# One weight item of each mixture loaded as one wide transfer and several eight-partition transfers

## The reference

```python
for e in range(N_EXPERTS):
    h = jax.nn.silu(t @ w_gate[e]) * (t @ w_up[e])
    y = y + combine[:, e:e + 1] * (h @ w_down[e]).astype(jnp.float32)
...
a = jax.nn.silu(jnp.einsum('becd,edf->becf', xs, w_gate)) * jnp.einsum('becd,edf->becf', xs, w_up)
y = jnp.einsum('becf,efd->becd', a, w_down) * g[..., None].astype(h.dtype)
```

## Time and profile before

| | us |
|---|---|
| median of 3 runs | 1846.8 (1843.21 to 1848.1) |
| the profiled execution, span from the first to the last instruction | 1843.4 |
| TensorE busy in it | 1431.2 |

### The profile page before, as it was taken

The page is one execution under the profiler, slowest core; times in us unless marked ns, Lnnn a source line. Parts: engine busy times, 40 slices in busy tenths (PEclk is TensorE's granted clock), DMA queues, the critical chain, the costliest instruction groups (busy, mean ns, idle before and its releaser), DMA issues.

```text
span 1843.4 us, 30528 instructions
## 1 busy us (share of the span) xinstructions
PE 1431.2 (78%) x13618; PEld 824.4 (45%) x13618; DVE 489.0 (27%) x999; ACT 245.8 (13%) x561; POOL 84.3 (5%) x92
## 2 busy tenths in 40 slices
PE   9999887776587999999666656678999756656666
PEld 5456442333243364666334334336867423434333
DVE  5864321111121169942000000004643100000000
ACT  3233210111211122411000000001001000000000
POOL 4100000000000042100000000000000000000000
PEclk9999998888899999999778778789999977887888
DMA  9665999999999996788999999999997999999997
GB/s 366 239 240 233 395 418 427 427 426 426 425 422 422 405 348 243 289 354 369 431 431 429 429 430 431 429 427 391 391 393 317 431 430 430 429 430 431 431 423 330
DMA packets 78031, 717.69 MB, mean 389 GB/s; under 512 B 5064, under 2 KB 9928, under 8 KB 48584
## 3 DMA queue, kind: packets, MB, share of 16 engines
q1 hardware_dynamic: 76336, 712.85, 93.0%
q10 hardware_dynamic: 1560, 2.82, 0.4%
HBM read 714.60 MB, written 1.05 MB: 388 GB/s over the span
## 4 chain that ended last, share of the span: by engine, by line
DMA 50%; PE 39%; DVE 5%; issue 2%; POOL 2%; ACT 1%; SPq 0%; ACTq 0%; DVEq 0%
DMA ring<-in_moe_w_down 33%; PE bank L1787 9%; DMA ring<-in_w_down 8%; PE bank L2680 5%; PE bank L535 4%; DMA ring<-in_attn_w_in 3%; PE bank L1729 3%; DMA ring<-in_moe_w_gate 2%; PE bank L1738 2%; PE bank L1047 2%; PE bank L1016 2%; PE bank L679 2%; DMA room<-in_rows 1%; PE bank L2440 1%; PE bank L1641 1%
## 5 line engine op out<-in xcount | busy, mean ns | idle before, releaser
L1738 PE MATMUL bank<-ring,arena 128*32 128x256 f32 x3840 | 288.2, 465 | 161.4 <-DMA ring<-in_moe_w_up 118.6
L1787 PE MATMUL bank<-ring,arena 128*32 128x256 f32 x2944 | 238.6, 486 | 138.8 <-DMA ring<-in_moe_w_down 113.1
L1738 PEld LDWEIGHTS bank<-ring,arena 128*32 128x32 f32 x3840 | 160.2, 132 | 285.2 <-issue 220.2
L1787 PEld LDWEIGHTS bank<-ring,arena 128*32 128x32 f32 x2944 | 123.7, 137 | 242.1 <-issue 193.1
L1729 PE MATMUL bank<-ring,arena 128*32 128x512 f32 x976 | 131.6, 661 | 64.6 <-ACT arena L1829 32.5
L1860 DVE TENSOR_TENSOR arena<-arena,bank 128x128 f32<-128x128 f32 (+1 forms) x64 | 22.7, 355 | 503.3 <-PE bank L1738 496.3
L535 PE MATMUL bank<-ring,low 128*128 128x512 f32 (+1 forms) x352 | 152.7, 581 | 0.1
L1815 PE MATMUL bank<-arena 32*128 32x256 f32 x1024 | 91.8, 428 | 15.0 <-PE bank L1815 10.6
L1871 ACT ACTIVATE arena<-bank 128x256 f32<-128x256 f32 x64 | 24.6, 385 | 556.6 <-PE bank L1801 554.3
L535 PEld LDWEIGHTS bank<-ring,low 128*128 128x128 f32 x352 | 64.9, 192 | 65.9 <-issue 65.0
L1729 PEld LDWEIGHTS bank<-ring,arena 128*32 128x32 f32 x976 | 27.5, 115 | 144.6 <-issue 63.9
(11 more groups left out here) (324 smaller groups left out, 1343.0 us busy)
## 6 DMA issues: line engine op xcount, KB each, us to landing
ring<-in_moe_w_gate SPq DMA_DIRECT2D x20, 4096.0 KB, 23.7
ring<-in_moe_w_up SPq DMA_DIRECT2D x20, 4096.0 KB, 23.7
ring<-in_moe_w_down SPq DMA_DIRECT2D x20, 4096.0 KB, 23.6
ring<-in_w_gate SPq DMA_DIRECT2D x31, 2048.0 KB, 22.6
ring<-in_w_up SPq DMA_DIRECT2D x30, 2048.0 KB, 23.8
ring<-in_w_down SPq DMA_DIRECT2D x30, 2048.0 KB, 24.5
ring<-in_ada_w SPq DMA_DIRECT2D x24, 2048.0 KB, 13.5
ring<-in_moe_w_up SPq DMA_DIRECT2D x22, 2048.0 KB, 20.8
```

The source lines that it names most:

```text
L1738: last = nc.tensor.matmul(GU[up][32 * j:32 * j + 32, 0:QW], xgT[:, x + kk, a:a + C], w[:, kq, j * QW:(j + 1) * QW], start=(kk == 0), stop= ...
L1787: last = nc.tensor.matmul(z_bank(M)[32 * j:32 * j + 32, 0:QW], act_s[:, kk, :], w[:, kq, j * QW:(j + 1) * QW], start=(kk == 0), stop=(kk = ...
```

## The change

In each mixture one gate item (expert 28 in stage 1, 8 in stage 2, 10 in stage 3) is no longer loaded by one transfer of 128 partitions. Partitions 0 to 79 (stage 1) or 0 to 95 (stages 2 and 3) go by one transfer, which counts up the slot's semaphore, and the rest by six or four transfers of eight partitions each, which count up `low_loaded`. This is the semaphore `half_loaded` under a second name, so the count that the last item waits for is raised. TensorE waits for both semaphores before the item's matmuls. The bytes moved are the same.

```diff
+LOW8 = {1: (28, 6), 2: (8, 4), 3: (10, 4)}
...
+        self.low_expert, self.low_parts = LOW8.get(stage, (None, 0))
...
+        low_loaded = half_loaded
+        low_at = [16 + 16 * sum(LOW8[n][1] for n in range(1, stage + 1)) for stage in range(4)]
+
+        def in_two(M, i):
+            return M.stage and i == place_up(M, M.low_expert, 0, 0)
+
+        def load_in_two(M, dst, src, landed):
+
+            at = P - 8 * M.low_parts
+            nc.sync.dma_start(dst[0:at], src[0:at]).then_inc(landed, 16)
+            for p in range(at, P, 8):
+                nc.sync.dma_start(dst[p:p + 8], src[p:p + 8]).then_inc(low_loaded, 16)
+
         def wait_moe_item(pe, M, i, r, k):
+            if in_two(M, i):
+                pe.wait_ge(low_loaded, low_at[M.stage])
...
-                    pe.wait_ge(half_loaded, 32)
+                    pe.wait_ge(half_loaded, low_at[3] + 16)
...
-                nc.sync.dma_start(ring[slot][:, :, :].rearrange("p a b -> p (a b)").rearrange("p (k n) -> p k n", n=rows_.shape[2]),
-                                  rows_).then_inc(M.arrived[slot], 16)
+                dst = ring[slot][:, :, :].rearrange("p a b -> p (a b)").rearrange("p (k n) -> p k n", n=rows_.shape[2])
+                if in_two(M, i):
+                    load_in_two(M, dst, rows_, M.arrived[slot])
+                    return
+                nc.sync.dma_start(dst, rows_).then_inc(M.arrived[slot], 16)
...
-                nc.sync.dma_start(slots.rearrange("p (k n) -> p k n", n=rows_.shape[2]), rows_).then_inc(arrived[at % SLOTS], 16)
+                dst = slots.rearrange("p (k n) -> p k n", n=rows_.shape[2])
+                if in_two(M, i):
+                    load_in_two(M, dst, rows_, arrived[at % SLOTS])
+                    return
+                nc.sync.dma_start(dst, rows_).then_inc(arrived[at % SLOTS], 16)
```

## The result

The kernel after takes 1911.3 us (median of 4 runs, 1908.4 to 1914.4) against 1846.1 us (median of 4 runs of the kernel before; three of them stood ahead of the prediction, with 1846.8), a ratio of 1.0353 with a 95% interval of 1.0339 to 1.0366. The prediction was 1840.1 us in a range of 1836.5 to 1850. Both the sign and the range are wrong. The profiled execution has a span of 1911.6 us, 68.2 longer than before.

A forecast was written before the change was run, and what follows sets the result against it. Each mixture was taken to last as long as its weights stream, ending with the more loaded DMA engines. 1.83 + 2.44 + 2.44 = 6.7 us off, costs 0.0, gave a 1836.7 us span and 1840.1 us median, range 1836.5 to 1850.

The forecast's parts named there:

- Engines and packets: Pair items in the mixtures: one 32 KB row is one packet, so an eight-row transfer occupies at most eight engines.
- The shift: Changed items: rows moved between engine halves at 26.9 or 25.6 GB/s per engine shift each engine by 1.83 or 2.44 us.
- The terms of 1.83, 2.44 and 2.44 us off: Ends of first, second and third mixture: each comes earlier by its shift, 6.7 us off together.
- The waits that were to end near 642.9 and 1256.7: TensorE's waits at the ends of the first two mixtures, before at 644.72 and 1260.96, would end earlier.
- Which half: Changed items: small transfers fall on the less loaded eight engines, taken by judgment; the other half would end 2.44 us later.
- rival A: Small transfers fall on engines that also fetch instructions; mixtures end 1.83, 2.44, 2.44 us later, 1853.5 us; chance 0.12.
- the light half: Eight of sixteen DMA engines, without instruction fetches, end the third mixture at about 1828.1, a gap of 5.3 us.
- The costs taken as nothing: Fourteen more SyncE issues, TensorE's second wait and added completion packets: -0.1 to +0.5 us in all, taken as 0.0.
- What follows the mixtures: Stretches behind the mixtures and the end after 1835.02 keep their length and only move with the mixtures' ends.
- Cover: DMA queue in the mixtures: 14 us of work stand ahead of an item, against a lead of 5.3 us.
- C: Small transfers are serialized: fourteen at some 2 us each add 28 us, 1875 us; chance 0.02.
- What would show it: Signs in the profile after: earlier wait ends and no half-share tail if right; other tails or share gaps if wrong.

The follow-up runs named there:

- patterns: Separate kernel without compute, loading weights in one row pattern after another, each alone and waited for: eight neighbouring rows 20.9 us, all 128 rows 41.3 us.
- step4_high: Against the changed kernel: small transfers into rows 96 to 127 take every fourth partition, four in every mixture; 1891.8 us, ratio 1.0253 to the kernel before.
- columns_pair: Against the kernel before: changed items cut by columns into two 128-partition transfers, three quarters and one quarter of each row; 1844.7 us, ratio 1.0003.
- stream_pieces: Separate kernel without compute, streaming a divided item among whole 128-row items: 68.0 us with the change's division, 41.2 us with four whole items.

## Why the prediction was wrong

**Engines and packets.** That an eight-row transfer is eight packets on at most eight engines was right. Completion packets are the short ones on the page: 5176 after, 5064 before, 112 more for fourteen more transfers, eight each.

**The shift, the step that failed.** "One engine moves 430 / 16 = 26.9 GB/s when all are busy and 205 / 8 = 25.6 in the tail ... so the shift is 1.83 us and 2.44 us for each engine." Both rates were read in transfers of 128 partitions and used for transfers of 8, 80 and 96. Nothing in the trace of before showed a large transfer of another shape in this queue, and the value should have had a bound from below as the issue cost had. Measured for the same bytes, in the stream: 21.9 us for the four small transfers, in place of 4.9 us of eight engines' time, and 14.6 us for rows 0 to 95, in place of 7.3. The terms of 1.83, 2.44 and 2.44 us off came out as 18.0 (with the stretch behind the first mixture), 21.5 and 27.0 us on. The waits that were to end near 642.9 and 1256.7 ended at 659.7 and 1300.5.

Behind the wrong rate stands a wrong picture. I treated the item as bytes that any engine can take from any other. By the map that `patterns` found, each group of rows has one way with one engine's rate, and a whole item already puts an equal load on every way. Rows given to other engines still go through the same ways, where the engines now meet. So moving rows makes no way's load lighter: it is eight rows for each whole item, whoever carries them. That is a conclusion from the map, not a run of its own; nor did a run try whether another engine could fill a way while the way's own engine fetches instructions. For the wide part, more than half of the price in `step4_high`, the picture is not complete: that it runs at half the rate is measured, why is open.

**Which half.** The whole forecast hung on it, by my words, and so did rival A with 0.12. No run settles which engines fetch instructions, since a shift of 2.4 us never showed under costs of 4 to 27. Whether the light half was the right guess stays open.

**The costs taken as nothing** were right: four issues 1.36 us, hidden behind queued work; the second wait, one more transfer and its completions 0 us (`columns_pair`). The completions of all fourteen were not tried by themselves. What follows the mixtures kept its length less well than I had it: the stretch behind the first grew by 3.0 us in 192, that behind the second by 1.6 in 136, and the last 8.4 us did not change.

**Cover.** "14 us of work stand ahead of it" held for gaps of 5 us. It does not cover an item that needs 27 us more of the queue itself: TensorE waited 22.76 us.

**The rivals.** C, at 0.02, had the right sign and place and a price of 28 us where 66.5 came in the three stage costs. Its mechanism, serialized fixed costs, is refuted by `columns_pair` and by step 4, which changed the price of the third mixture at the same number of transfers (27.0 to 18.1). I dismissed it since "the mixtures stream one item after another at 430 GB/s"; they do so with whole items only. The Trainium skill's rule cited there (DMA: Bandwidth & Descriptors, section "Rules for kernel authors": use one 128-partition transfer rather than two to disjoint halves, which serialize) was good advice here, and the trace agrees: in `patterns` each half took 43.6 us by itself, the two issued together 84.2, all 128 rows in one transfer 41.3. I had taken from it only a fixed cost for each transfer and left out that each half by itself runs at half the rate.

**What would show it.** "Gaps of 1 to 2 us in the share at the changed items (C)" would have missed it: the share had no gap. The rate beside the share shows it.

## What to carry to other kernels

A rate belongs to the shape of the transfer it was read in. Before a stream of 128-partition transfers is cut by partitions, price the new shape by itself: here a 96-row part of an item took 1.5 times as long as the whole item, and eight neighbouring rows moved 50 GB/s, the rate of two engines; a cut along the columns cost nothing. And read the GB/s line together with the DMA share: 0.85 at 125 GB/s was a queue full of slow transfers, which the share alone does not tell from a good stream.

## What the runs showed of the hardware

- Eight rows of 128 KB: 20.9 us as neighbours, 12.7 with step 2, 7.6 with step 4, 12.6 with step 16; the order in on-chip memory counts, not that in the source (20.6 and 7.4 with the two exchanged).
- Rows of 128 KB by number: 32 spread rows 12.5 us, 32 neighbours 22.5 and 22.7, 64 rows 43.6, 128 rows 41.3, all by the load of the busiest way. More than that load explains: 48 rows (80 to 127) and 80 rows (0 to 79) 52.4 each, 96 rows 63.1 (0 to 95) and 62.7 (32 to 127), 112 rows 65.4. Engines that meet one after the other on several ways might do that; it was not tried by itself and stays open.
- Small transfers into rows 96 to 127 cost the stream 4 to 6 us more than the same ones into rows 0 to 31 (53.8 against 49.5, 41.9 against 36.3). In the second pair 1 MB into rows 0 to 31 adds 4.5 us, about what eight engines need at 26.9 GB/s each (4.9); why rows 96 to 127 take 10.1 is open.
- An eight-row issue on SyncE took 0.27 to 0.47 us for neighbours, mostly 0.30, and 0.61 to 0.79 us with a step (`patterns` and `stream_pieces`).
